# Feed-forward chunks 1 to 9 with the weights stationary and all 256 tokens moving

## The chip, the cores and the metric

One core of one Trainium2 chip. The metric is the device time of one execution in microseconds, as the median of several runs of the same program.

## The reference, cut to what matters

A two-layer decoder trunk on 256 tokens of width 1024. Four of its eight stages are half-step SwiGLU feed-forwards with an inner width of 2816, and these are what the change touches:

```python
def swiglu(x, w_gate, w_up, w_down):
    return (jax.nn.silu(x @ w_gate) * (x @ w_up)) @ w_down

x = layer_norm(DN_ALPHA * x + 0.5 * swiglu(x, ffn_w_gate[i, 0], ffn_w_up[i, 0], ffn_w_down[i, 0]),
               ln_g[i, 0], ln_b[i, 0])
```

The stages are, in order: feed-forward, attention (8 MoBA and 8 forgetting heads), feed-forward, gated input embedding; feed-forward, spatial gating unit (SGU), feed-forward, gated input embedding. All data are float32.

## The kernel before

**Numbers.** Products run in the `fp32r` format. To keep float32 accuracy each operand is split into a high part (ScalarE copies it into an `fp32r` tile) and a low part (VectorE subtracts the high part from the original), and each product is three matmuls: high with high, high with low, low with high (`product`, L332 to L334). This holds for activations (`xT_hi`, `xT_lo`), for h (`hT_hi`, `hT_lo`) and for every weight (`g_hi`, `g_lo`, `d_hi`, `d_lo`).

**Tiling of a feed-forward.** The inner width is cut into 11 chunks of 256 features (`NCH`, `FC`). For one chunk a weight tile of 1024 x 512 is loaded: 256 columns of the gate weight beside 256 of the up weight. It comes in two halves of the contraction (`rawA` for blocks 0 to 3, `rawB` for blocks 4 to 7), and the 256 x 1024 tile of the down weight comes into `rawD`. SyncE issues these loads in a fixed order and waits before each until VectorE has read the raw tile (`load_half`, `load_d`). The split weights have two slots each, so they are made one chunk ahead.

**One chunk on TensorE** (`chunk`, L436). Tokens are stationary: for each half h of 128 tokens, `up` runs 8 blocks x 3 matmuls with `xT` as weights of 128 x 128 and 512 moving columns (gate beside up) into PSUM bank `gu[h]`. So `gu[h]` is tokens by features. ScalarE takes silu of its first 256 columns (`gate`, L725), VectorE multiplies this by 0.5 and by the other 256 columns (`gated`, L995) into `stage`. The down product contracts over features, so h must be turned: `turn` transposes two blocks of 128 x 128 of `stage` into PSUM bank `tp[h]` (L385), ScalarE makes the high part from there (`hT_high`), VectorE the low part (`hT_low`), and `down` (12 matmuls of 512 columns for each half of the tokens) adds into `acc[h]`.

**Order.** All orders are written by hand, and semaphores tie the engines. On TensorE a chunk is

```python
up(c, cs, 0)
turn(c - 1, cs - 1, 1)
down(c - 1, cs - 1, 0)
up(c, cs, 1)
turn(c, cs, 0)
down(c - 1, cs - 1, 1)
```

so the down product runs one chunk behind. ScalarE runs, in a chunk: the high part of the next chunk's rawA, `gate` of half 0, `hT_high` of half 1 of the chunk before, the high part of rawD, that of rawB, `gate` of half 1, `hT_high` of half 0. VectorE runs in the same order the low parts and `gated`. Chunks 0 and 10 are partly written out: chunk 0 meets the end of the stage before, chunk 10 the layer norm behind it. Chunks 2 to 9 are hardware loops of two chunks each. In the second feed-forward of each layer, `p_tok` is transposed once, through the same `tp` banks.

**Counting.** `phase_bases` gives for each stage how often each semaphore has been raised before it; `turn` and `hT_high` compute their waits from these.

## Time and profile before

| | |
|---|---|
| median of 3 runs | 1067.05 us |
| lowest, highest run | 1065.72, 1068.27 us |
| span of the profiled execution | 1064.0 us |
| instructions | 12641 |
| mean granted clock of TensorE | 0.982 of full |
| HBM read | 189.90 MB, 179 GB/s over the span |

The profile is of one execution. Its span runs from the first to the last instruction and is 3.05 us below the median of the runs; the page gives no other time of that execution. PE is TensorE's matmuls, PEld its weight loads (recorded apart, since they overlap the matmuls), DVE VectorE, ACT ScalarE, POOL GpSimd, SP SyncE. L332 is line 332 of the kernel. Matmul ends are modelled and matmuls overlap, so what one costs in a stream is the distance from start to start, not its recorded duration.

### The profile page before, as it was taken

To read this page: it belongs to the slowest core of one execution; us is meant where nothing else is said; L and a number is where in the kernel's file an instruction comes from. 1 tells how busy PE (TensorE), PEld (TensorE's weight loads), DVE (VectorE), ACT (ScalarE), POOL (GpSimd) and SP (SyncE) were. 2 spreads that over 40 slices of the span, in tenths; PEclk is the share of its full clock that TensorE was granted. 3 is DMA by queue.
4 is the path that set the end of the run, shared out by engine and by line. 5 is a ranking of instruction groups with operands and counts; after the bars stand their busy time and mean duration, and the time that the engine had idled before them with its cause. 6 is when DMAs were issued, how large, how long until landed. Compare 5 with 4: busy or idle time off the path is not lost.

```text
span 1064.0 us, 12641 instructions
## 1 busy us (share of the span) xinstructions
PE 1044.0 (98%) x4770; PEld 856.1 (80%) x4770; DVE 610.9 (57%) x704; ACT 447.3 (42%) x515; POOL 39.4 (4%) x53
## 2 busy tenths in 40 slices
PE   7999999999999899999999999999999899999998
PEld 5888888787878688888888888888888788888886
DVE  4554455775434855445586554545678775454574
ACT  5434344345533553434435444344354454444441
POOL 2100000100000100000010000000110100000010
PEclk9999999999967999999999999999999999999999
DMA  8854656355312475565546755546266575654531
GB/s 281 286 197 158 207 179 207 116 161 160 118 41 70 173 271 198 160 212 181 183 170 222 249 178 183 197 158 209 87 208 236 178 258 192 203 188 167 197 119 40
DMA packets 128882, 191.46 MB, mean 180 GB/s; under 512 B 5288, under 2 KB 95400, under 8 KB 128720
## 3 DMA queue, kind: packets, MB, share of 16 engines
q1 hardware_dynamic: 125920, 180.37, 50.3%
q0 software_dynamic: 2928, 10.61, 3.0%
q8 instruction: 24, 0.39, 0.1%
q14 instruction: 10, 0.08, 0.0%
HBM read 189.90 MB, written 1.06 MB: 179 GB/s over the span
## 4 chain that ended last, share of the span: by engine, by line
PE 91%; DVE 4%; DMA 2%; ACT 1%; issue 1%; SPq 0%; POOL 0%; DVEq 0%
PE gu L332 19%; PE gu L334 19%; PE gu L333 19%; PE acc L332 9%; PE acc L334 9%; PE acc L333 9%; PE tp L385 4%; DVE g_lo L896 2%; PE acc L527 2%; ACT g_hi L675 1%; DMA rawB<-in_ffn_w_up 1%; DMA rawB<-in_sgu_w_in 1%; PE acc L524 1%; DMA rawB<-in_sgu_w_out 0%; DVE xT_lo L896 0%
## 5 line engine op out<-in xcount | busy, mean ns | idle before, releaser
L332 PE MATMUL gu<-g_hi,xT_hi 128*128 128x512 f32 x928 | 365.0, 393 | 5.9 <-DVE xT_lo L896 2.9
L334 PE MATMUL gu<-g_hi,xT_lo 128*128 128x512 f32 x928 | 362.2, 390 | 0.0
L333 PE MATMUL gu<-g_lo,xT_hi 128*128 128x512 f32 x928 | 361.8, 390 | 0.0
L332 PEld LDWEIGHTS gu<-g_hi,xT_hi 128*128 128x128 f32 x928 | 174.6, 188 | 43.5 <-DVE xT_lo L896 3.3
L334 PEld LDWEIGHTS gu<-g_hi,xT_lo 128*128 128x128 f32 x928 | 174.6, 188 | 36.6
L333 PEld LDWEIGHTS gu<-g_lo,xT_hi 128*128 128x128 f32 x928 | 174.8, 188 | 35.6 <-issue 0.2
L725 ACT ACTIVATE stage<-gu 128x256 f32<-128x256 f32 x88 | 33.8, 384 | 377.7 <-PE gu L334 377.7
L896 DVE TENSOR_TENSOR g_lo<-rawA,g_hi 128x2048 fp32r<-128x2048 f32 (+1 forms) x63 | 142.1, 2256 | 85.1 <-ACT g_hi L675 85.1
L896 DVE TENSOR_TENSOR g_lo<-rawB,g_hi 128x2048 fp32r<-128x2048 f32 x62 | 141.7, 2286 | 19.4 <-ACT g_hi L675 19.2
L995 DVE SCALAR_TENSOR_TENSOR stage<-stage,gu 128x256 f32<-128x256 f32 x88 | 37.0, 420 | 193.8 <-ACT stage L725 193.6
L332 PE MATMUL acc<-d_hi,hT_hi 128*128 128x512 f32 x352 | 144.4, 410 | 0.0
L675 ACT ACTIVATE g_hi<-rawA 128x2048 fp32r<-128x2048 f32 (+1 forms) x63 | 119.0, 1888 | 51.6 <-DMA rawA<-in_ffn_w_up 29.1
L334 PE MATMUL acc<-d_hi,hT_lo 128*128 128x512 f32 x352 | 138.0, 392 | 0.0
L333 PE MATMUL acc<-d_lo,hT_hi 128*128 128x512 f32 x352 | 137.7, 391 | 0.0
L896 DVE TENSOR_TENSOR d_lo<-rawD,d_hi 128x2048 fp32r<-128x2048 f32 x46 | 105.4, 2291 | 48.5 <-ACT d_hi L675 48.5
L675 ACT ACTIVATE g_hi<-rawB 128x2048 fp32r<-128x2048 f32 x62 | 118.6, 1913 | 11.4 <-DMA rawB<-in_ffn_w_up 5.1
L675 ACT ACTIVATE d_hi<-rawD 128x2048 fp32r<-128x2048 f32 x46 | 88.2, 1917 | 4.0 <-PE acc L334 2.6
L334 PEld LDWEIGHTS acc<-d_hi,hT_lo 128*128 128x128 f32 x352 | 66.1, 188 | 14.2
L333 PEld LDWEIGHTS acc<-d_lo,hT_hi 128*128 128x128 f32 x352 | 66.4, 189 | 11.5
L332 PEld LDWEIGHTS acc<-d_hi,hT_hi 128*128 128x128 f32 x352 | 66.2, 188 | 11.2
L1317 POOL TENSOR_TENSOR small<-small 128x1 f32<-128x1 f32 x14 | 18.0, 1287 | 940.2 <-DVE small L931 940.2
L896 DVE TENSOR_TENSOR hT_lo<-tp,hT_hi 128x256 fp32r<-128x256 f32 x88 | 36.9, 419 | 9.7 <-ACT hT_hi L675 9.7
(159 smaller groups left out, 703.7 us busy)
## 6 DMA issues: line engine op xcount, KB each, us to landing
rawD<-in_ffn_w_down SPq DMA_DIRECT2D x44, 1024.0 KB, 4.8
rawB<-in_ffn_w_gate SPq DMA_DIRECT2D x44, 512.0 KB, 4.1
rawB<-in_ffn_w_up SPq DMA_DIRECT2D x44, 512.0 KB, 5.3
rawA<-in_ffn_w_gate SPq DMA_DIRECT2D x43, 512.0 KB, 3.8
rawA<-in_ffn_w_up SPq DMA_DIRECT2D x43, 512.0 KB, 4.7
rawA<-in_attn_w_in SPq DMA_DIRECT2D x12, 512.0 KB, 4.4
rawB<-in_attn_w_in SPq DMA_DIRECT2D x12, 512.0 KB, 4.6
rawA<-in_ple_w_gate SPq DMA_DIRECT2D x8, 512.0 KB, 5.4
```

The lines of the kernel that those rows point to most:

```text
L332: pe.matmul(dst, hi[b], w_hi[b], start=first and b == 0, stop=False)
L333: pe.matmul(dst, hi[b], w_lo[b], start=False, stop=False)
L334: done = pe.matmul(dst, lo[b], w_hi[b], start=False, stop=last and b == len(hi) - 1)
L385: done = pe.transpose(tp[bank][0:src.shape[1], rows * q:rows * q + rows], src, ident[0:rows, 0:rows])
L524: pe.matmul(acc[0][:, sl, 0:S + P], sel_r[:, hh * P:hh * P + P], c_part[:, :], start=start, stop=False)
L527: done = pe.matmul(acc[0][:, sl, cols], qT[rows, blk, i_q * P:i_q * P + P], kT[rows, blk, 0:cols.stop - cols.start], start=g == 0, stop=g ...
L675: return act.activation(dst, src, ACT.Copy, scale=scale)
L725: act.activation(stage[:, h, 0:FC], gu[h][:, 0:FC], ACT.Silu).then_inc(act_done, 1)
L896: return dve.tensor_tensor(dst, src, hi.bitcast(F32), ALU.subtract)
L995: dve.scalar_tensor_tensor(out=stage[:, h, FC:2 * FC], in0=stage[:, h, 0:FC], scalar=0.5, in1=gu[h][:, FC:2 * FC], op0=ALU.mult, op1=ALU.m ...
L1317: pool.tensor_tensor(rstd[:, h:h + 1], var_eps[:, h:h + 1], neg_half, ALU.pow)\
```

## The change

In chunks 1 to 9 the roles in the first product are exchanged. The weights are stationary (128 of their columns at a time) and all 256 tokens move (`up_w`): `gu[0]` then holds the gate product and `gu[1]` the up product, each as two blocks of 128 features by 256 tokens. ScalarE takes silu of the whole `gu[0]` (`gate_w`), VectorE multiplies it by 0.5 and by `gu[1]` (`gated_w`) into `stage`, which is then features by tokens; the high and low parts of h are made from `stage` in SBUF (`hw_high`, `hw_low`) without a transpose. `up_w` runs 48 matmuls of 256 moving columns for each of its two calls in a chunk. Chunks 0 and 10 stay as they were. `hT_hi` and `hT_lo` have two slots of 256 tokens; `causal_c`, used in the attention alone, shares its place with `hT_hi`. The diff, cut to its core:

```diff
@@ -93,11 +92,11 @@
-    per = {"ffn": dict(g=NCH, d=NCH, u=NCH, t=NCH + 2, v=NCH + 2, a=2 * NCH, x=4, r=4, ln=1),
-           "attn": dict(g=8, d=0, u=6, t=5 + HEADS + 1 + 2, v=3, a=0, x=8, r=4, ln=1),
-           "sgu": dict(g=6, d=0, u=4, t=2 + 2, v=4, a=8, x=8, r=4, ln=2),
-           "ple": dict(g=2, d=1, u=2, t=2, v=2, a=4, x=4, r=0, ln=0)}
-    now = dict(g=0, d=0, u=0, t=2, v=2, a=0, x=0, r=0, ln=0)
+    per = {"ffn": dict(g=NCH, d=NCH, u=NCH, t=4, v=4, a=4, x=4, r=4, ln=1, hw=NCH - 2),
+           "attn": dict(g=8, d=0, u=6, t=5 + HEADS + 1 + 2, v=3, a=0, x=8, r=4, ln=1, hw=0),
+           "sgu": dict(g=6, d=0, u=4, t=2 + 2, v=4, a=8, x=8, r=4, ln=2, hw=0),
+           "ple": dict(g=2, d=1, u=2, t=2, v=2, a=4, x=4, r=0, ln=0, hw=0)}
+    now = dict(g=0, d=0, u=0, t=2, v=2, a=0, x=0, r=0, ln=0, hw=0)
     out = []
     for kind, _, s in PHASES:
         out.append(dict(now))
...
@@ -142,8 +141,13 @@
         xT_hi = sb("xT_hi", [P, KB, S], F32R)
         xT_lo = sb("xT_lo", [P, KB, S], F32R)
         stage = sb("stage", [P, HALVES, 512])
-        hT_hi = sb("hT_hi", [P, 3, 2, P], F32R)
-        hT_lo = sb("hT_lo", [P, 3, 2, P], F32R)
+        with ExitStack() as region:
+            hT_hi = sb("hT_hi", [P, 2, 2, S], F32R, region)
+        with ExitStack() as region:
+            causal_c = sb("causal_c", [P, 2, 384], where=region)
+        h_end = sb("h_tail", [P, 4 * S])
+        del h_end
+        hT_lo = sb("hT_lo", [P, 2, 2, S], F32R)
         pT_hi = sb("pT_hi", [P, HALVES, 2, P], F32R)
         pT_lo = sb("pT_lo", [P, HALVES, 2, P], F32R)
         gamma = sb("gamma", [P, D])
...
@@ -413,33 +417,50 @@
             for k, (kind, i, s) in enumerate(PHASES):
                 B = bases[k]
-                g0, d0, u0, t0, x0, a0 = (B[q] for q in ("g", "d", "u", "t", "x", "a"))
+                g0, d0, u0, t0, x0, a0, w0 = (B[q] for q in ("g", "d", "u", "t", "x", "a", "hw"))
                 if kind == "ffn":
...
                         g_product(g0 + c, (g0 + cs) % 2, h, gu[h][:, :], between=between)
-                    def turn(c, cs, h):
-                        pe.wait_ge(gu_taken[h], u0 + c + 1)
-                        transposes(h, t0 + c + p_use(s, cs, h), [stage[:, h, FC + P * b:FC + P * b + P] for b in range(2)])
+                    def up_w(c, cs, q):
+                        n, slot = g0 + c, (g0 + cs) % 2
+                        bank_free(q, u0 + c)
+                        for b in range(2):
+                            cols, dst = slice(FC * q + P * b, FC * q + P * b + P), gu[q][:, S * b:S * b + S]
+                            for kb in range(KB):
+                                if b == 0 and q == 0 and kb % 4 == 0:
+                                    pe.wait_ge((split_a, split_b)[kb // 4], n + 1)
+                                pe.matmul(dst, g_hi[:, slot, kb, cols], xT_hi[:, kb, :], start=kb == 0, stop=False)
+                                pe.matmul(dst, g_lo[:, slot, kb, cols], xT_hi[:, kb, :], start=False, stop=False)
+                                done = pe.matmul(dst, g_hi[:, slot, kb, cols], xT_lo[:, kb, :], start=False,
+                                                 stop=kb == KB - 1)
+                        done.then_inc(g_done, 1)
+                    def turn(n, h):
+                        pe.wait_ge(gu_taken[h], u0 + (1, NCH)[n])
+                        transposes(h, t0 + n * (1 + p_use(s)), [stage[:, h, FC + P * b:FC + P * b + P] for b in range(2)])
                     def down(c, cs, h, js=(0, 1)):
-                        pe.wait_ge(tp_taken[h], t0 + c + (2 if s == 2 and cs >= 1 else 1))
+                        if cs in (0, NCH - 1):
+                            pe.wait_ge(tp_taken[h], t0 + (1 if cs == 0 else 2 + p_use(s)))
+                        else:
+                            pe.wait_ge(hw_lo, w0 + c)
                         if k == 0 and cs == 0 and h == 1:
                             pe.wait_ge(bias_sb, 1)
-                        at = 2 if h == 1 and cs == NCH - 1 else h
-                        d_product(d0 + c, (d0 + cs) % 2, h, hT_hi[:, at], hT_lo[:, at], first=cs == 0,
-                                  last=cs == NCH - 1, js=js)
+                        tok = slice(h * P, (h + 1) * P)
+                        d_product(d0 + c, (d0 + cs) % 2, h, hT_hi[:, cs % 2, :, tok], hT_lo[:, cs % 2, :, tok],
+                                  first=cs == 0, last=cs == NCH - 1, js=js)
                     def chunk(c, cs):
-                        up(c, cs, 0)
-                        turn(c - 1, cs - 1, 1)
+                        up_w(c, cs, 0)
+                        if cs == 1:
+                            turn(0, 1)
                         down(c - 1, cs - 1, 0)
-                        up(c, cs, 1)
-                        turn(c, cs, 0)
+                        up_w(c, cs, 1)
                         down(c - 1, cs - 1, 1)
                     xT_wait(0, use)
...
@@ -468,17 +489,16 @@
                     c = NCH - 1
                     up(c, c, 0)
-                    turn(c - 1, c - 1, 1)
                     down(c - 1, c - 1, 0)
-                    turn(c, c, 0)
+                    turn(1, 0)
                     bank_free(1, u0 + c)
...
                     down(c - 1, c - 1, 1, (0,))
-                    turn(c, c, 1)
+                    turn(1, 1)
                     down(c - 1, c - 1, 1, (1,))
-                    use = (t0 + NCH + p_use(s, c, 0), t0 + NCH + p_use(s, c, 1) + 1)
+                    use = (t0 + 2 + p_use(s), t0 + 3 + p_use(s))
                     ln_turn(0, x0, use)
                     down(c, c, 1)
...
@@ -716,13 +737,21 @@
             for k, (kind, i, s) in enumerate(PHASES):
                 B = bases[k]
-                g0, d0, u0, t0, x0, a0 = (B[q] for q in ("g", "d", "u", "t", "x", "a"))
+                g0, d0, u0, t0, x0, a0, w0 = (B[q] for q in ("g", "d", "u", "t", "x", "a", "hw"))
                 last_phase = k + 1 == len(PHASES)
                 if kind == "ffn":
-                    def gate(c, h, value=None):
-                        act.wait_ge(g_done, 2 * c + (2 * g0 + h + 1))
+                    def gate(c, h):
+                        act.wait_ge(g_done, 2 * (g0 + c) + h + 1)
                         act.activation(stage[:, h, 0:FC], gu[h][:, 0:FC], ACT.Silu).then_inc(act_done, 1)
+                    def gate_w(c):
+                        act.wait_ge(g_done, 2 * c + (2 * g0 + 1))
+                        act.activation(stage[:, 0, :], gu[0][:, :], ACT.Silu).then_inc(gu_taken[0], 1)
+                    def hw_high(c, cs):
+                        act.wait_ge(gu_taken[1], u0 + c + 1)
+                        copy(hT_hi[:, cs % 2, :, :], stage[:, 1, :].rearrange("p (b t) -> p b t", b=2)).then_inc(hw_hi, 1)
                     def chunk(c, cs):
                         slot = (g0 + cs + 1) % 2
...
@@ -731,19 +760,25 @@
                         hi_g_into(c + (g0 + 1), slot, 0)
                         if k > 0 and cs == 0:
                             half1()
-                        gate(c, 0)
+                        if cs == 0:
+                            gate(c, 0)
+                        elif cs == 1:
+                            hT_high(1, 0, t0)
                         if cs > 0:
-                            hT_high(1, c + (t0 - 1 + p_use(s, cs - 1, 1)))
+                            gate_w(c)
                         hi_d(c + d0, (d0 + cs) % 2)
                         hi_g_into(c + (g0 + 1), slot, 1)
-                        gate(c, 1)
-                        hT_high(0, c + (t0 + p_use(s, cs, 0)))
+                        if cs == 0:
+                            gate(c, 1)
+                            hT_high(0, 0, t0)
+                        else:
+                            hw_high(c, cs)
                     chunk(0, 0)
...
                         for h in range(HALVES):
-                            act.wait_ge(tp_full[h], t0 + 3 - h)
+                            act.wait_ge(tp_full[h], t0 + 2)
                             copy(pT_hi[:, h, :, :], tp[h][:, 0:2 * P].rearrange("p (b t) -> p b t", b=2))\
                                 .then_inc(tp_hi[h], 1)
                     with act.Fori(0, (NCH - 3) // 2) as r:
...
@@ -985,16 +1019,28 @@
                 B = bases[k]
                 f0 = sum(kind in ("ffn", "ple") for kind, _, _ in PHASES[:k])
-                g0, d0, u0, t0, v0, a0, x0, r0, ln0 = (B[q] for q in ("g", "d", "u", "t", "v", "a", "x", "r", "ln"))
+                g0, d0, u0, t0, v0, a0, x0, r0, ln0, w0 = (
+                    B[q] for q in ("g", "d", "u", "t", "v", "a", "x", "r", "ln", "hw"))
                 last_phase = k + 1 == len(PHASES)
                 if kind == "ffn":
                     def gated(c, h):
-                        dve.wait_ge(act_done, 2 * c + (a0 + h + 1))
+                        dve.wait_ge(act_done, a0 + (2 if c else 0) + h + 1)
                         dve.scalar_tensor_tensor(out=stage[:, h, FC:2 * FC], in0=stage[:, h, 0:FC], scalar=0.5,
                                                  in1=gu[h][:, FC:2 * FC], op0=ALU.mult, op1=ALU.mult)\
                             .then_inc(gu_taken[h], 1)
+                    def gated_w(c):
+                        dve.wait_ge(gu_taken[0], u0 + c + 1)
+                        dve.wait_ge(g_done, 2 * c + (2 * g0 + 2))
+                        dve.scalar_tensor_tensor(out=stage[:, 1, :], in0=stage[:, 0, :], scalar=0.5, in1=gu[1][:, :],
+                                                 op0=ALU.mult, op1=ALU.mult).then_inc(gu_taken[1], 1)
+                    def hw_low(c, cs):
+                        dve.wait_ge(hw_hi, w0 + c)
+                        low(hT_lo[:, cs % 2, :, :], stage[:, 1, :].rearrange("p (b t) -> p b t", b=2),
+                            hT_hi[:, cs % 2, :, :]).then_inc(hw_lo, 1)
                     def chunk(c, cs):
                         slot = (g0 + cs + 1) % 2
...
@@ -1008,13 +1054,16 @@
                             if k > 0:
                                 half1()
                             gated(c, 0)
-                        if cs > 0:
-                            gated(c, 0)
-                            hT_low(1, c + (v0 - 1 + p_use(s, cs - 1, 1)))
+                        if cs == 1:
+                            hT_low(1, 0, v0)
                         lo_d(c + d0, (d0 + cs) % 2)
                         lo_g_into(c + (g0 + 1), slot, 1)
-                        gated(c, 1)
-                        hT_low(0, c + (v0 + p_use(s, cs, 0)))
+                        if cs == 0:
+                            gated(c, 1)
+                            hT_low(0, 0, v0)
+                        else:
+                            gated_w(c)
+                            hw_low(c, cs)
                     chunk(0, 0)
                     if k == 0:
```

## Rows read from the trace of the kernel before

**Rows 1.** The page: engine table, then the chain that ended last by engine

```profile
PE 1044.0 (98%) x4770; PEld 856.1 (80%) x4770; DVE 610.9 (57%) x704; ACT 447.3 (42%) x515; POOL 39.4 (4%) x53
...
PE 91%; DVE 4%; DMA 2%; ACT 1%; issue 1%; SPq 0%; POOL 0%; DVEq 0%
```

**Rows 2.** Stretches: a chunk, the attention heads (busy by engine, granted clock, DMA)

```profile
core 0: us, PE busy (x) PEld busy (x) DVE busy (x) ACT busy (x) POOL busy (x), PEclk, DMA share, GB/s
...
162.22:179.05 16.83, 16.83 (x78) 13.87 (x77) 8.30 (x8) 6.72 (x7) 0.00 (x0) 1.00 0.57 190
...
299.00:334.00 35.00, 34.95 (x123) 28.55 (x123) 11.94 (x51) 12.76 (x39) 0.00 (x0) 0.51 0.00 1
```

**Rows 3.** Groups by form, TensorE: busy us, mean ns of one | idle before

```profile
L332 PE MATMUL gu<-g_hi,xT_hi 128*128 128x512 f32 x928 | 365.0, 393 | 5.9 <-DVE xT_lo L896 2.9 <-DVE g_lo L896 2.9
...
L332 PE MATMUL acc<-d_hi,hT_hi 128*128 128x512 f32 x352 | 144.4, 410 | 0.0
...
L385 PE MATMUL tp<-ident,stage 128*128 128x128 f32 x208 | 38.2, 271 | 0.0
...
L332 PEld LDWEIGHTS gu<-g_hi,xT_hi 128*128 128x128 f32 x928 | 174.6, 188 | 43.5 <-DVE xT_lo L896 3.3 <-DVE g_lo L896 2.6 <-issue 2.1
```

**Rows 4.** In order of time, TensorE, one chunk: start us, us

```profile
162.22 0.39 PE L332 MATMUL gu<-g_hi,xT_hi 128*128 128x512 f32 x1
...
167.43 0.39 PE L334 MATMUL gu<-g_hi,xT_lo 128*128 128x512 f32 x1
...
168.11 0.39 PE L333 MATMUL acc<-d_lo,hT_hi 128*128 128x512 f32 x1
168.34 0.40 PE L334 MATMUL acc<-d_hi,hT_lo 128*128 128x512 f32 x1
168.58 0.39 PE L332 MATMUL acc<-d_hi,hT_hi 128*128 128x512 f32 x1
...
179.04 0.39 PE L332 MATMUL gu<-g_hi,xT_hi 128*128 128x512 f32 x1
```

**Rows 5.** In order of time, TensorE, forget-gate product

```profile
218.61 0.28 PE L332 MATMUL acc<-xT_hi,wf_hi 128*8 128x256 f32 x1
...
219.29 0.28 PE L332 MATMUL acc<-xT_hi,wf_hi 128*8 128x256 f32 x1
```

**Rows 6.** In order of time, weight loads: after a turn, and in the SGU

```profile
108.88 0.19 PEld L332 LDWEIGHTS acc<-d_hi,hT_hi 128*128 128x128 f32 x1
108.99 0.19 PEld L333 LDWEIGHTS acc<-d_lo,hT_hi 128*128 128x128 f32 x1
...
812.56 1.87 PEld L621 LDWEIGHTS acc<-v_sgu,ws_T 128*128 128x128 f32 x16
```

**Rows 7.** Groups by form, VectorE and ScalarE: 128x256 beside 128x512

```profile
L995 DVE SCALAR_TENSOR_TENSOR stage<-stage,gu 128x256 f32<-128x256 f32 x88 | 37.0, 420 | 193.8 <-ACT stage L725 193.6
...
L725 ACT ACTIVATE stage<-gu 128x256 f32<-128x256 f32 x88 | 33.8, 384 | 377.7 <-PE gu L334 377.7
...
L1072 DVE TENSOR_TENSOR stage<-stage,acc 128x512 f32<-128x512 f32 x8 | 5.5, 684 | 12.8 <-PE acc L334 7.9 <-ACT stage L781 4.9
...
L781 ACT ACTIVATE stage<-gu 128x512 f32<-128x512 f32 x8 | 4.8, 598 | 36.9 <-PE gu L334 36.9
```

**Rows 8.** In order of time: low parts of rawB, a third-phase chunk's first matmul

```profile
172.56 2.29 DVE L896 TENSOR_TENSOR g_lo<-rawB,g_hi 128x2048 fp32r<-128x2048 f32 x1
...
587.49 2.28 DVE L896 TENSOR_TENSOR g_lo<-rawB,g_hi 128x2048 fp32r<-128x2048 f32 x1
...
588.72 0.48 PE L332 MATMUL gu<-g_hi,xT_hi 128*128 128x512 f32 x1
```

**Rows 9.** In order of time, TensorE: scores of three attention heads

```profile
297.04 0.92 PE L527 MATMUL acc<-kT,qT 64*128 64x256 f32 x4
...
299.52 1.54 PE L527 MATMUL acc<-kT,qT 64*128 64x256 f32 x4
...
303.93 0.79 PE L527 MATMUL acc<-kT,qT 64*128 64x256 f32 x1
```

More of the change, by code:

```diff
@@ L456, in _ @@
                                   stop=True).then_inc(bias_mm, 1)
-                    turn(0, 0, 0)
+                    turn(0, 0)
                     chunk(1, 1)
@@ L461, in _ @@
                         for h in range(HALVES):
-                            transposes(h, t0 + 2 - h, [p_tok[:, h, P * b:P * b + P] for b in range(2)])
+                            transposes(h, t0 + 1, [p_tok[:, h, P * b:P * b + P] for b in range(2)])
                     with pe.Fori(0, (NCH - 3) // 2) as r:
```

33 lines of the change are left out of this document (16 added, 17 removed).

## The prediction

> **What bounds the kernel now.** I read the page first: its engine table gives TensorE 98% of a span of 1064.0 us, and the chain that ended last is 91% TensorE [rows 1]. A busy TensorE isn't TensorE at its peak, so the second view is the stretch view with the granted clock. In a whole feed-forward chunk the clock is full (2.4 GHz) and the engine never idle; only in the attention heads is about half of it granted (0.51, the 1.2 GHz level) [rows 2]. The groups by form give what the engine does: 928 triples of weight products and 352 triples of down products, each matmul 512 moving columns, and 208 transposes of `stage` [rows 3]. Their mean of 390 ns is not what one costs, since they overlap. So the fourth view is the order of time: one chunk from the first matmul of its up product at 162.22 to that of the next at 179.04 lasts 16.82 us, and the 24 matmuls of one up product start from 162.22 to 167.43, which is 5.21 / 23 = 0.2267 us from start to start [rows 4]. A chunk has 48 + 24 = 72 of these, 16.32 us. The remaining 0.50 us is its four transposes. One turn can be seen alone: the last up matmul starts at 167.43, two transposes follow, and the second down matmul starts at 168.11 [rows 4]. That is 0.68 us for what is two steps of 0.2267 without the turn, so a turn costs 0.23; twice that is 0.46, and the last 0.04 lies in the spacings of the down product behind it, up to 0.24 at 168.34 and 168.58 [rows 4]. There is no idle time in the chunk, so each nanosecond of TensorE's stream is a nanosecond of the span.
>
> **The change part by part.** Removed: chunks 1 to 9 have 18 of the 22 turns of a feed-forward phase; chunks 0 and 10 keep four. Nine chunks in each of four phases are 36, and 36 x 0.50 us = 18.0 us leave TensorE's stream. Nothing else hides there, so I count all of it.
>
> Changed: in those chunks 48 up matmuls of 512 moving columns become 96 of 256. The columns are the same, the weight loads double. Over the kernel 36 x 48 = 1728 matmuls become 3456. What a 256-column matmul in this number format costs can be read off the forget-gate product: its matmuls start at 218.61 and, six later, at 219.29, so 0.1133 us each [rows 5], exactly half of 0.2267. If that holds, 3456 x 0.1133 = 391.7 us take the place of 1728 x 0.2267 = 391.7, and the cost is nothing. But those matmuls load 8 weight columns, the new ones 128. What hides the load is the matmul before it, and that cover shrinks from 0.227 to 0.113 us. How fast can loads of 128 columns follow each other? The SGU's matmuls (128 moving columns) show it: sixteen loads span 1.87 us, and one lasts about 0.19, so (1.87 - 0.19) / 15 = 0.112 us from one to the next [rows 6]. After a turn, the load for the first down matmul starts at 108.88 and the next at 108.99, 0.11 us later, although such a load is recorded as 188 ns [rows 3, 6]. So the load just fits: 0.112 under 0.1133, with a margin of about one nanosecond. The low bound of the price is 0.1133, since half a 512-column matmul can't stream faster than it does now. The high bound, if a load must finish its recorded 188 ns before its matmul starts and the next load only starts with that matmul, is 0.188 us. Between these I take 0.1136, nearest to rows 5, as the two rates are too close for none of the pairs to slip: 3456 x 0.0003 = +1.0 us.
>
> Here a rule of the Trainium skill speaks against the change. The page Perfetto Trace Analysis, section Identifying the Most-Contended Engine, says to judge how near TensorE is to its limit by the busy share of its weight loads. That share is 80% [rows 1], and 1728 loads more of 188 ns would add 325 us to 856 us, more than the span. By it the loads would become the bound; the sum goes by the starts, which are closer together than the loads are long.
>
> VectorE and ScalarE: a chunk's two silu of 384 ns become one of about 598 (the 128x512 sigmoid row), its two gatings of 420 ns one of about 684 (a 128x512 product with PSUM); the two high copies and the two low parts of h shrink likewise, so each engine is some 0.3 us a chunk shorter [rows 7]. Neither engine is the bound. The path to h is new: after the second up product, gating, high copy, low part, about 0.68 + 0.60 + 0.68 = 2.0 us with hand-offs on top. The down product that needs it comes after the previous chunk's second down half (12 x 0.2267 = 2.7) and the next first up product (5.4), so 8.1 us cover it. ScalarE now waits for the gating ahead of its next high copy of weights, and VectorE for the high copy ahead of its next low part, some 1.5 us later than before. The first half's low part is ready before that of the second half starts at 172.56, for a chunk that begins at 179.04 [rows 4, 8], so at least 6.5 us early: it can take that. PSUM banks come free as before, since each is read within a microsecond and not rewritten for a half chunk. The loads that SP issues are the same in number and order; SP waits for the same low parts, and POOL's queue is untouched. The overlay of `causal_c` moves no instruction.
>
> One requirement comes sooner: the second half of the weights (rawB) is needed after 12 matmuls of the first up product, which is 2.72 us now and 1.36 us then. In a steady chunk the low part ends at 174.85 and is needed at 179.04 + 2.72 = 181.76, 6.9 us of slack [rows 8]. The tightest is chunk 1 of the third feed-forward phase: ready at 589.77, needed at 588.72 + 1.36 = 590.08, so 0.3 us remain [rows 8]. I cost this at nothing; were that cover gone, it would cost some tenths of a microsecond, four times at most.
>
> Sum: -18.0 + 1.0 = -17.0 us. The profiled execution spans 1064.0 us and so becomes 1047.0. The page gives no time of that execution beyond its span; the three timed runs have a median of 1067.05, 3.05 us over it, which I leave as it is: 1050.0 us, -1.6%.
>
> **The rivals.** (a) The loads slip a little. If the 17/16 by which moving columns fall short of 2.4 GHz (0.2267 us against 512 / 2.4 = 0.2133) also stretches a load, 0.112 becomes 0.117 us. That is 3456 x 0.0037 = 12.8 us given back: -18.0 + 12.8 gives 1061.9 us. For it: the margin is a nanosecond, and loads then run under every matmul. Against it: 0.112 was measured with loads and matmuls running together.
>
> (b) Slower: the weight load ends last at every pair. Its place is the hand-over from load to matmul in the 96 up matmuls of a chunk; the load starts only when the matmul before it has started, and every delay of it then shows. It decides from 18.0 us / 3456 = 5.2 ns a pair, at 0.1185 us. Spacings disturbed by this much exist: behind a turn down matmuls start 0.23 to 0.24 us apart instead of 0.2267 [rows 4]. If each pair had 7 ns more, it would be 0.120 us, +24.2 us: 1067.05 - 18.0 + 24.2 = 1073.2 us. Against it: with 512 columns a load has more than twice the cover, and the disturbed spacings still come only behind a turn, so they aren't the load's own length.
>
> (c) The loads bind at their recorded length: 3456 x (0.188 - 0.1133) = +258 us, 1307 us. Loads that follow each other in 0.11 us [rows 6] speak clearly against it. This is what the Trainium skill's rule (Perfetto Trace Analysis, Identifying the Most-Contended Engine) would mean here.
>
> (d) The gain is paid back elsewhere: the second half of the weights is late in every chunk, or the attention heads lose clock. A head starts 2.48 us after the one before at the full level (297.04 to 299.52) and 4.41 us at the half one (299.52 to 303.93) [rows 9]; the heads will now come 4.5 us earlier (nine chunks of the first phase), and the fall of the clock may catch one head more or fewer, 2 us either way. That belongs to the forecast's own range. As a rival, all of it together taking back 18 us, it gives about 1067 us; nothing speaks for it.
>
> **How the numbers follow.** Forecast 0.70, at 1046.5 to 1054 (2 us either way for the clock, 1.3 for the spread of the runs, and up to 1 ns a pair). Rival (a) 0.13, 1054 to 1065. Rival (b) 0.12. Rival (c) 0.02. Rival (d) 0.03, within 0.2%, which is about what a measurement of this kernel can tell from no change (2 us of 1067). A tail of (a) ends in that band too, so: faster 0.82, same 0.04, slower 0.14. The range 1046.5 to 1065 takes in the forecast and (a), and leaves (b), (c) and the edges out.
>
> **What the changed profile would show.** Right: 208 transposes of `stage` become 64; 96 matmuls of 128x256 in a chunk, starting 0.113 us apart; a chunk period of 16.3 us; 1728 loads more, whose busy share nears 100% without the span growing; VectorE idle before its gating until the second up product ends. Wrong: starts 0.117 us or more apart at full clock (a, b); gaps ahead of the 13th of the 256-column matmuls with VectorE's low part of rawB as releaser (d); a granted clock below 1.00 in feed-forward chunks.

## The result and the profile after

| | before | after |
|---|---|---|
| median | 1067.12 us (4 runs) | 1072.95 us (4 runs) |
| lowest, highest | 1065.72, 1068.27 us | 1071.73, 1075.38 us |
| ratio after / before, 95% interval | | 1.0069, 1.0051 to 1.0088 |
| span of the profiled execution | 1064.0 us | 1069.6 us |

The change makes the kernel 0.5 to 0.9% slower, where 1.6% faster was forecast. The page of the changed kernel, its engine table and its chain, answers to [rows 1]:

```profile
PE 1049.1 (98%) x6354; PEld 933.1 (87%) x6354; DVE 606.3 (57%) x632; ACT 442.5 (41%) x443; POOL 38.9 (4%) x53
...
PE 90%; DVE 5%; DMA 2%; issue 1%; ACT 1%; POOL 0%; SPq 0%; DVEq 0%; ACTq 0%
```

Little of the kernel waits anew: TensorE is still 98% busy and 90% of the chain. The weight loads rose from 80% to 87%, not towards 100%. So most of the loss must be inside TensorE's own stream. Groups by form (busy us, mean ns of one | idle before), against [rows 3]:

```profile
L437 PE MATMUL gu<-xT_hi,g_hi 128*128 128x256 f32 x1152 | 326.3, 283 | 1.2 <-DVE g_lo L930 1.2
...
L389 PE MATMUL tp<-ident,stage 128*128 128x128 f32 x64 | 10.9, 272 | 0.0
...
L437 PEld LDWEIGHTS gu<-xT_hi,g_hi 128*128 128x128 f32 x1152 | 220.8, 192 | 4.2 <-DVE g_lo L930 1.7
```

The 256-column matmuls are there, 3 x 1152. The idle time ahead of them is 1.2 us in the whole kernel. In order of time, the first and last of the 48 matmuls of one `up_w` call, then the first matmuls of two chunks that follow each other (start us, us), against [rows 4]:

```profile
103.66 0.28 PE L437 MATMUL gu<-xT_hi,g_hi 128*128 128x256 f32 x1
...
109.30 0.28 PE L439 MATMUL gu<-xT_lo,g_hi 128*128 128x256 f32 x1
...
112.16 0.28 PE L437 MATMUL gu<-xT_hi,g_hi 128*128 128x256 f32 x1
...
129.16 0.28 PE L437 MATMUL gu<-xT_hi,g_hi 128*128 128x256 f32 x1
```

From 112.16 to 129.16 the chunk period is 17.00 us, where 16.3 was forecast. The 48 matmuls start from 103.66 to 109.30: 5.64 / 47 = 0.120 us each, not 0.1136. Thirty-six chunks times (17.00 - 16.82) are 6.5 us.

There is one new wait, in chunk 1 of the second feed-forward and in the same way in that of the fourth. The 12th and 13th matmuls of the second feed-forward's chunk 1, and the low part of rawB that the 13th needs:

```profile
373.01 0.28 PE L439 MATMUL gu<-xT_lo,g_hi 128*128 128x256 f32 x1
373.90 0.39 PE L437 MATMUL gu<-xT_hi,g_hi 128*128 128x256 f32 x1 [0.61 <-DVE g_lo L930]
...
371.56 2.29 DVE L930 TENSOR_TENSOR g_lo<-rawB,g_hi 128x2048 fp32r<-128x2048 f32 x1
```

The low part ends at 373.85, and the 13th matmul starts 0.89 us after the 12th instead of 0.12. The fourth feed-forward loses 0.80 us in the same place, so the two waits cost 1.6 us. The spans differ by 5.6 us and not by 6.5 + 1.6, since other parts of the kernel became shorter: from the first feed-forward's last chunk to the second one's chunk 1, where the attention heads lie, it is 191.5 us (180.16 to 371.62) against 193.0 (179.04 to 372.01).

The path to h, in order of time on VectorE and ScalarE, and the first down matmul that reads it:

```profile
109.62 0.69 DVE L1037 SCALAR_TENSOR_TENSOR stage<-stage,gu 128x512 f32<-128x512 f32 x1 [1.57 <-PE gu L439]
...
110.34 0.63 ACT L695 ACTIVATE hT_hi<-stage 128x512 fp32r<-128x512 f32 x1 [5.02 <-DVE stage L1037]
...
111.00 0.69 DVE L930 TENSOR_TENSOR hT_lo<-stage,hT_hi 128x512 fp32r<-128x512 f32 x1 [0.70 <-ACT hT_hi L695]
...
117.92 0.40 PE L336 MATMUL acc<-d_hi,hT_hi 128*128 128x512 f32 x1
```

Gating, high copy and low part end at 111.69, 2.4 us after the last matmul of `up_w` started at 109.30. The down product that reads them begins behind the next `up_w`, at 117.92, another 6.2 us later. This part of the prediction held.

### The profile page after: what moved, and what is told of

Its sections match the earlier page's. It is cut to its first block, busy times and chain, and to the rows that moved or that the text cites. A ratio compares the mean times of both kernels' runs of the same rounds, so it can differ in the third digit from the quotient of the medians.

```text
span 1069.6 us, 15501 instructions
## 1 busy us (share of the span) xinstructions
PE 1049.1 (98%) x6354; PEld 933.1 (87%) x6354; DVE 606.3 (57%) x632; ACT 442.5 (41%) x443; POOL 38.9 (4%) x53
## 3 DMA queue, kind: packets, MB, share of 16 engines
HBM read 189.90 MB, written 1.06 MB: 179 GB/s over the span
## 4 chain that ended last, share of the span: by engine, by line
PE 90%; DVE 5%; DMA 2%; issue 1%; ACT 1%; POOL 0%; SPq 0%; DVEq 0%; ACTq 0%
PE gu L437 13%; PE gu L439 13%; PE gu L438 13%; PE acc L336 9%; PE acc L337 9%; PE acc L338 8%; PE gu L336 7%; PE gu L338 6%; PE gu L337 6%; PE tp L389 2%; DVE g_lo L930 2%; PE acc L547 1%; DMA rawB<-in_ffn_w_up 1%; DMA v_att<-bias_rows 1%; DVE x_tok L982 1%
## 5 line engine op out<-in xcount | busy, mean ns | idle before, releaser
L437 PE MATMUL gu<-xT_hi,g_hi 128*128 128x256 f32 x1152 | 326.3, 283 | 1.2 <-DVE g_lo L930 1.2
L439 PE MATMUL gu<-xT_lo,g_hi 128*128 128x256 f32 x1152 | 326.0, 283 | 0.0
L438 PE MATMUL gu<-xT_hi,g_lo 128*128 128x256 f32 x1152 | 325.9, 283 | 0.0
L437 PEld LDWEIGHTS gu<-xT_hi,g_hi 128*128 128x128 f32 x1152 | 220.8, 192 | 4.2 <-DVE g_lo L930 1.7
L438 PEld LDWEIGHTS gu<-xT_hi,g_lo 128*128 128x128 f32 x1152 | 220.9, 192 | 2.6
L439 PEld LDWEIGHTS gu<-xT_lo,g_hi 128*128 128x128 f32 x1152 | 220.8, 192 | 0.0
L336 PE MATMUL gu<-g_hi,xT_hi 128*128 128x512 f32 x352 | 140.5, 399 | 5.6 <-DVE xT_lo L930 2.9
L338 PE MATMUL gu<-g_hi,xT_lo 128*128 128x512 f32 x352 | 138.0, 392 | 0.0
L337 PE MATMUL gu<-g_lo,xT_hi 128*128 128x512 f32 x352 | 137.7, 391 | 0.0
L695 ACT ACTIVATE g_hi<-rawB 128x2048 fp32r<-128x2048 f32 x62 | 118.2, 1907 | 9.2 <-DMA rawB<-in_ffn_w_up 3.2
L338 PEld LDWEIGHTS gu<-g_hi,xT_lo 128*128 128x128 f32 x352 | 66.5, 189 | 14.3
```

What stands on the lines that cost most here:

```text
L336: pe.matmul(dst, hi[b], w_hi[b], start=first and b == 0, stop=False)
L337: pe.matmul(dst, hi[b], w_lo[b], start=False, stop=False)
L338: done = pe.matmul(dst, lo[b], w_hi[b], start=False, stop=last and b == len(hi) - 1)
L437: pe.matmul(dst, g_hi[:, slot, kb, cols], xT_hi[:, kb, :], start=kb == 0, stop=False)
L438: pe.matmul(dst, g_lo[:, slot, kb, cols], xT_hi[:, kb, :], start=False, stop=False)
L439: done = pe.matmul(dst, g_hi[:, slot, kb, cols], xT_lo[:, kb, :], start=False, stop=kb == KB - 1)
```

## The experiments

Each ratio is against runs of the kernel before on the same chip. e3, e4, e6 and e9 are one execution each and are read for the distances between starts alone.

**e1: tokens stationary again, no turning.** Only the first product of the changed kernel is put back; silu, gating and down product then take `gu` unturned, so the output means nothing.

```diff
-                        for b in range(2):
...
+                        tok = slice(q * P, (q + 1) * P)
+                        for kb in range(KB):
...
+                            done = product(gu[q][:, :], [xT_hi[:, kb, tok]], [xT_lo[:, kb, tok]],
+                                           [g_hi[:, slot, kb, :]], [g_lo[:, slot, kb, :]], kb == 0, kb == KB - 1)
```

> The changed kernel with the first product of chunks 1 to 9 put back to tokens stationary and 512 weight columns moving, while its new path without transposes stays: the two terms of the sum taken apart. What it leaves out is the turning of h: silu, gating and down product take gu as it comes, so the numbers mean nothing, but every operation of the changed kernel has its size. Theory A (the loss is the weight load under a 256-column matmul, 120.0 ns from start to start in the changed trace against 113.3, 3456 x 6.7 ns = 23.0 us): the load is hidden again, so the time is the changed kernel's less 23.0 us, 1072.95 - 23.0 = 1050.0 us, a chunk period of 16.32 us. Theory B (taking the transposes away did not give its 18.0 us, or the new path to h waits somewhere): 1055 us or more, with idle time ahead of the down products or a period over 16.5 us.

Measured: 1042.93 us, ratio 0.9789 (0.9768 to 0.9811), so 22.5 us faster than before, and 30 faster than the changed kernel, not 23. The first matmuls of two chunks that follow each other, in order of time:

```profile
100.24 0.39 PE L336 MATMUL gu<-g_hi,xT_hi 128*128 128x512 f32 x1
...
116.56 0.39 PE L336 MATMUL gu<-g_hi,xT_hi 128*128 128x512 f32 x1
```

The stretch from 290 to 345 us (the last three numbers are the granted clock, the share of the DMA engines and GB/s):

```profile
290.00:345.00 55.00, 52.98 (x237) 43.51 (x237) 28.68 (x79) 21.77 (x51) 1.00 (x1) 0.78 0.13 44
```

The period is 16.32 us, exactly the forecast: the transposes' 0.50 us a chunk did leave, 18.0 us in all, and no wait took their place. The spans of the two profiled executions, 1064.0 and 1039.4 us, differ by 24.6 us; most of the rest is the clock. The granted clock of the stretch above, which holds the attention heads, is 0.78; the same stretch has 0.69 in the kernel before and 0.72 in the changed one. Nine hundredths of 55 us at half speed are 2 x 0.09 x 55 = 9.9 us fewer at 1.2 GHz, and a head needs 2.48 us at full and 4.41 at half level [rows 9], so by estimate 9.9 us cost 9.9 x (1 - 2.48 / 4.41) = 4.3 us. 18.0 + 4.3 is 22.3 of the 24.6; from 10 to 25 us the granted clock is 1.00 here and 0.89 before, which can hold part of what is left. The medians differ less than the spans, because the clock also varies from run to run: over a whole execution it is 0.984 to 0.989 in the four runs of e1 and 0.978 to 0.984 in the 17 of the kernel before.

Against the changed kernel the chunks alone give 36 x (17.00 - 16.32) = 24.5 us, near the 23.0 of theory A, and the two waits of 1.6 us are gone. Six hundredths of granted clock are worth 2.9 us by the same estimate; that makes 29.0 of the 30. Theory B falls.

**e10: one thing alone.** The kernel before, with each 512-column matmul of the first product in chunks 1 to 9 split into two of 256. Nothing else changes.

```diff
+                        for b in range(2):
+                            half = slice(FC * b, FC * b + FC)
+                            for kb in range(KB):
...
+                                done = product(gu[h][:, half], [xT_hi[:, kb, tok]], [xT_lo[:, kb, tok]],
+                                               [g_hi[:, slot, kb, half]], [g_lo[:, slot, kb, half]],
+                                               first=kb == 0, last=kb == KB - 1)
```

> The kernel before with one thing alone: in chunks 1 to 9 each 512-column matmul of the first product becomes two of 256 columns (all 24 of the gate columns, then all 24 of the up columns). Tokens stay stationary, h is turned as before, the reference is computed. Theory E (each matmul carries about 13.3 ns beyond its columns at 2.4 GHz once 128 columns are loaded for it, in this orientation too): 120 ns from start to start, a chunk period of 16.83 + 48 x 0.0133 = 17.47 us, and 1728 x 0.0133 = 23.0 us more, 1088.5 to 1090 us. Theory of the prediction (time goes by columns alone, 113.3 ns): no change, 1066 to 1067 us.

Measured: 1085.48 us, ratio 1.0201 (1.0171 to 1.0231). The ratio stands for 21.4 us more, the medians (1066.19 us before on that chip) for 19.3. First and last of 48 matmuls, and the first of the next chunk:

```profile
105.43 0.28 PE L332 MATMUL gu<-g_hi,xT_hi 128*128 128x256 f32 x1
...
111.06 0.28 PE L334 MATMUL gu<-g_hi,xT_lo 128*128 128x256 f32 x1
...
122.88 0.28 PE L332 MATMUL gu<-g_hi,xT_hi 128*128 128x256 f32 x1
```

5.63 / 47 = 0.120 us, with tokens stationary and the weights moving; the period is 122.88 - 105.43 = 17.45 us, 0.63 over [rows 4] and 17.47 by theory E. Thirty-six times 0.63 are 22.7 us. The total is some 3 us under the 1088.5 expected: the two waits of 1.6 us are here too, but the granted clock from 290 to 345 us is 0.78 against 0.69, worth 4.3 us by the estimate in e1. 22.7 + 1.6 - 4.3 is 20.0, and the spans differ by 19.1 (1083.1 against 1064.0). The prediction's own theory, no change, falls. The split alone costs what the changed kernel lost. The roles of the operands have no part in it.

**e3: how it goes with the moving columns.** The number of columns that move differs by feed-forward phase.

```diff
+                                nm = {0: 128, 2: 192, 4: 320, 6: 384}[k]
+                                hi = xT_hi[:, :, :].rearrange("p k t -> p (k t)")[:, at:at + nm]
```

> One look at starts. In chunks 1 to 9 the number of moving columns differs by feed-forward phase: 128, 192, 320 and 384 in place of 256; what it leaves out or doubles are tokens, so the output means nothing. Theory A (a load of 128 columns takes about 117 ns from the start of the matmul before, whatever moves): 120 ns from start to start at 128 and 192 columns, and 141.7 and 170.0 ns at 320 and 384 (columns x 0.4427 ns, nothing added). Theory C (a fixed 6.7 ns a matmul on top of its columns): 63, 92, 148 and 177 ns. Theory D (the load is slowed by the columns that move beside it): about 112 ns at 128 columns, as the SGU's matmuls had it, and 120 at 192.

First and last of 48 matmuls, for each of the four widths:

```profile
100.58 0.22 PE L442 MATMUL gu<-xT_hi,g_hi 128*128 128x128 f32 x1
...
105.77 0.28 PE L444 MATMUL gu<-xT_lo,g_hi 128*128 128x128 f32 x1
...
439.84 0.25 PE L442 MATMUL gu<-xT_hi,g_hi 128*128 128x192 f32 x1
...
445.07 0.27 PE L444 MATMUL gu<-xT_lo,g_hi 128*128 128x192 f32 x1
...
665.45 0.30 PE L442 MATMUL gu<-xT_hi,g_hi 128*128 128x320 f32 x1
...
672.34 0.31 PE L444 MATMUL gu<-xT_lo,g_hi 128*128 128x320 f32 x1
...
969.45 0.33 PE L442 MATMUL gu<-xT_hi,g_hi 128*128 128x384 f32 x1
...
977.62 0.33 PE L444 MATMUL gu<-xT_lo,g_hi 128*128 128x384 f32 x1
```

So 5.19 / 47 = 0.110 and 5.23 / 47 = 0.111 us at 128 and 192 columns, 6.89 / 47 = 0.1466 at 320, 8.17 / 47 = 0.1738 at 384. From 256 columns (120.0 ns) to 512 (226.7 ns [rows 4]) each column adds 106.7 / 256 = 0.417 ns, one period of 2.4 GHz. Take off the columns at that rate (133.3 and 160.0 ns) and 13.3 and 13.8 ns are left at 320 and 384. At 512 it is 226.7 - 213.3 = 13.3 ns, at 256 it is 120.0 - 106.7 = 13.3 ns. From 256 to 512 columns one law fits all four widths, in streams of equal matmuls that load 128 columns each: **columns / 2.4 GHz plus 13.3 ns a matmul.** Theory A falls twice: the loads can follow each other in 0.111 us, less than 0.120, and at 320 and 384 the extra time is there although the load has ample cover. Theory C's form, a fixed cost on top, is right from 256 columns up, but with 13.3 ns over the columns at 2.4 GHz instead of 6.7 over columns of 0.4427 ns; below, starts follow the loads at 0.11 us. Theory D had that for 128 columns and missed it at 192, where it said 0.120.

**e4: how it goes with the loaded columns.** 256 columns move; 124, 120, 64 and (128, 64, 128) are loaded. Features are left out.

> One look at starts. In chunks 1 to 9, 256 columns move as in the changed kernel, but the number of stationary columns differs by feed-forward phase: 124, 120, 64, and in the last phase 128, 64, 128 over the three matmuls. The features of the columns left out are not computed. Theory A (the load is bound by its columns, some 0.83 to 0.89 ns each): 116.5 ns from start to start at 124 columns, 113.3 at 120 (load and moving columns level) and 113.3 at 64; in the last phase 113.3 into the matmul that loads 64, and 120 into the two that load 128. Theory C (fixed overhead): 120 ns in all four phases.

First and last of 48 matmuls in the first and third phase:

```profile
102.52 0.28 PE L440 MATMUL gu<-xT_hi,g_hi 128*124 128x256 f32 x1
...
108.03 0.28 PE L444 MATMUL gu<-xT_lo,g_hi 128*124 128x256 f32 x1
...
657.25 0.28 PE L440 MATMUL gu<-xT_hi,g_hi 128*64 128x256 f32 x1
...
662.58 0.28 PE L444 MATMUL gu<-xT_lo,g_hi 128*64 128x256 f32 x1
```

5.51 / 47 = 0.117 us at 124 loaded columns, and by the same count 0.117 at 120 (second phase) and 5.33 / 47 = 0.1135 at 64; the last phase, with one load in three of 64 columns, has 0.1166. So part of the fixed cost belongs to the load, and with 64 columns half of it is gone, as it was with the 8 columns of [rows 5]. But 120 and 124 columns cost the same, which a load bound by its columns would not: theory A has 0.1133 at 120. Theory C, 0.120 in all four phases, is wrong in all four.

**e6: roles, order, and few loaded columns.** By phase: tokens stationary with 256 weight columns moving; the same stationary twice in a row; 64 loaded and 512 moving; 32 loaded and 256 moving. Operands are left out or doubled.

> One look at starts, by feed-forward phase, in chunks 1 to 9 (the output means nothing: features, tokens or low parts are left out or doubled). First phase: tokens stationary again, but the weights move in pieces of 256 columns. Second: as in the changed kernel, the two products with the same stationary g_hi behind each other. Third: 64 stationary columns and 512 moving. Fourth: 32 stationary columns and 256 moving. Theory E (about 13.3 ns on top of columns / 2.4 GHz with 128 columns loaded, 6.7 with 64 or fewer, whatever moves): 120, 120, 220 and 113.3 ns from start to start. Theory G (the cost is tied to this orientation or to a change of weights): 113.3 ns in the first or in every third start of the second. Theory H (what a load adds shows only under short matmuls): 226.7 ns in the third.

The first two phases gave 0.120. First and last of 48 matmuls in the third and fourth:

```profile
710.42 0.40 PE L456 MATMUL gu<-g_hi 128*64 128x512 f32 x1
...
721.23 0.39 PE L456 MATMUL gu<-g_lo,g_hi 128*64 128x512 f32 x1
...
1026.22 0.28 PE L456 MATMUL gu<-xT_hi,g_hi 128*32 128x256 f32 x1
...
1031.75 0.28 PE L456 MATMUL gu<-xT_lo,g_hi 128*32 128x256 f32 x1
```

10.81 / 47 = 0.230 us, against 0.220 expected, and 5.53 / 47 = 0.118 against 0.113. Theories G and H fall. Theory E is right in the first two phases and wrong in the last two: fewer loaded columns do not always shorten the cost. With 256 moving, 32 were slower than 64, and with 512 moving, 64 (0.230) were slower than 128 (0.2267 [rows 4]).

**e9: data and banks.** By phase: no accumulation; moving tokens 16 columns later; two PSUM banks by turns; one and the same pair of operands throughout.

> One look at starts, by feed-forward phase, all with 128 columns loaded and 256 moving (the output means nothing). First phase: no accumulation, every matmul starts afresh in PSUM. Second: the moving tokens begin 16 columns later. Third: matmuls go by turns to a bank of gu and of tp. Fourth: every matmul loads the same 128 columns and moves the same 256. Theory E (the 120 ns belong to loading 128 columns under 256 moving ones, not to data or banks): 120 ns in all four. Theory L (adding to what the last matmul wrote costs it): 113.3 in the first and third. Theory M (the two reads of SBUF collide by address): other than 120 in the second or fourth.

0.120 us in the first, third and fourth phase. First and last of 48 matmuls in the first and second:

```profile
104.41 0.28 PE L449 MATMUL gu<-xT_hi,g_hi 128*128 128x256 f32 x1
...
110.05 0.28 PE L449 MATMUL gu<-xT_lo,g_hi 128*128 128x256 f32 x1
...
449.52 0.28 PE L449 MATMUL gu<-xT_hi,g_hi 128*128 128x256 f32 x1
...
455.09 0.29 PE L449 MATMUL gu<-xT_lo,g_hi 128*128 128x256 f32 x1
```

Neither adding to the last result nor the bank has a part, nor a change of operands, so theory L falls. Moving the read by 16 columns gives 5.57 / 47 = 0.1185 instead of 0.120: the place in SBUF counts, for about 1.5 ns. Theory M has that much right, and theory E, 0.120 throughout, misses it.

**e2, e5, e8: fewer matmuls for the same columns.** If each matmul has a fixed cost, the two that share g_hi should be one. It moves xT_hi beside xT_lo (512 columns); VectorE adds the halves of the bank.

```diff
-                                pe.matmul(dst, g_hi[:, slot, kb, cols], xT_hi[:, kb, :], start=kb == 0, stop=False)
-                                pe.matmul(dst, g_lo[:, slot, kb, cols], xT_hi[:, kb, :], start=False, stop=False)
-                                done = pe.matmul(dst, g_hi[:, slot, kb, cols], xT_lo[:, kb, :], start=False,
+                                pe.matmul(gu[b][:, :], g_hi[:, slot, kb, cols], xT_both[:, :, kb, :], start=kb == 0,
+                                          stop=False)
+                                done = pe.matmul(gu[b][:, 0:S], g_lo[:, slot, kb, cols], xT_hi[:, kb, :], start=False,
...
+                            dve.tensor_reduce(stage[:, q, S * b:S * b + S], gu[b][:, :].rearrange("p (r t) -> p t r", r=2),
+                                              AXX, ALU.add).then_inc(m_read, 1)
```

> A version that computes the reference: in chunks 1 to 9 the two products with g_hi become one matmul of 512 moving columns (xT_hi beside xT_lo in one tile), and the product with g_lo stays at 256 columns. A feature block takes a whole PSUM bank and VectorE adds its two halves (four reductions of 128x512 a chunk). Theory A (a load of 128 columns needs about 117 ns and shows only under a matmul of 256 columns): of three slots of 120 ns remain one of 120 and one of 226.7, 346.7 instead of 360.0 ns for each of 1152 triples, so 15.4 us less than the changed kernel: 1072.95 - 15.4 = 1057.6 us, faster than both. Theory C (every matmul of weights stationary carries 6.7 ns, whatever it moves): 120.0 + 233.3 = 353.3 ns, 1065.3 us. If VectorE with about 2.7 us more a chunk comes late, TensorE waits for banks and the time is above 1060 us under both.

Measured: 1066.49 us, ratio 1.0003 (0.9991 to 1.0016). Two of the pairs in order of time, with the first matmul of the pair after the third, and VectorE's reductions ahead of them and behind them:

```profile
107.49 0.40 PE L441 MATMUL gu<-xT_both,g_hi 128*128 128x512 f32 x1
107.72 0.28 PE L443 MATMUL gu<-xT_both,g_lo 128*128 128x256 f32 x1
107.84 0.40 PE L441 MATMUL gu<-xT_both,g_hi 128*128 128x512 f32 x1
108.08 0.28 PE L443 MATMUL gu<-xT_both,g_lo 128*128 128x256 f32 x1
...
108.55 0.40 PE L441 MATMUL gu<-xT_both,g_hi 128*128 128x512 f32 x1
...
102.49 0.69 DVE L1051 TENSOR_REDUCE stage<-gu 128x256 f32<-128x512 f32 x1 [1.57 <-PE gu L443]
...
110.10 1.47 DVE L1051 TENSOR_REDUCE stage<-gu 128x256 f32<-128x512 f32 x2
```

The group by form of the 512-column ones (busy us, mean ns | idle before, and for what):

```profile
L441 PE MATMUL gu<-xT_both,g_hi 128*128 128x512 f32 x1152 | 410.6, 399 | 3.1 <-DVE stage L1051 1.8 <-DVE g_lo L935 1.3
```

Three pairs take 1.06 us (107.49 to 108.55), so a pair takes 353 ns, not 346.7: better than the 360 of three matmuls, but the law doesn't hold for a mix. (The expectations below speak of 236.6 and 118.5 ns, 355 together; these are means over all calls and hold the waits of chunk 1 too.) Theory A falls. Theory C's 353.3 ns fit, but e3 has shown its sum wrong, so the right number speaks for nothing. TensorE also waited 1.8 us for VectorE's reductions in chunk 1 and 1.3 us for the low part of rawB.

e5 put the two runs of 256 columns next to each other in SBUF:

> The merged version again (it computes the reference), with xT_hi and xT_lo side by side for each block, so that the 512 moving columns are one contiguous run instead of two runs of 256. In the first merged version that matmul took 236.6 ns to the next start, not 226.7, and the 256-column one 118.5. Theory E (each matmul costs its columns at 2.4 GHz and about 13.3 ns on top when 128 columns are loaded for it; two separate runs in a moving operand cost 10 ns more): 226.7 + 120 = 346.7 ns a triple instead of 355, a chunk period of 16.5 us instead of 16.77, and 36 x 0.27 = 9.6 us less than the first merged version: about 1057 us. Theory F (the 236.6 comes from VectorE's reductions reading PSUM beside the matmuls, not from the operand's shape): no change, 1066 us.

Measured: 1067.32 us, ratio 1.0003 (0.9988 to 1.0018), with the distances of e2 within 0.1 ns. Theory E's part on two runs falls. Theory F has the right time, but e2's trace speaks against its cause: no reduction runs from 103.18 to 110.10, and the three pairs from 107.49 on take their 1.06 us all the same. e8 ordered the matmuls in groups of four of a kind, with the wait for the reductions in chunk 1 taken out (the 1.3 us for rawB stay):

> The merged version with the two kinds of matmul no longer alternating: four of 512 columns with g_hi, then four of 256 with g_lo, twice for each feature block. VectorE's first two reductions of chunk 1 also go ahead of its low part of rawA, since in the last version TensorE waited there 1.4 us in the first phase and 0.85 us in the second for a bank. It computes the reference. Theory I (the 236.5 ns of the 512-column matmul comes from standing between 256-column ones: the load for its successor and its own columns get in each other's way once for each change of size): inside a group 226.7 and 120 ns return, 346.7 on average, a chunk period of 16.5 to 16.6 us, and 6 to 10 us less with the two waits another 2 us less: 1056 to 1060 us. Theory K (the sum per 768 columns is what it is, 355 ns, however they are ordered): period 16.77, and only the waits are gained, 1065 us.

Measured: 1062.04 us, ratio 0.9963 (0.9945 to 0.9981). The first matmuls of two chunks that follow each other:

```profile
102.71 0.39 PE L443 MATMUL gu<-xT_both,g_hi 128*128 128x512 f32 x1
...
119.42 0.39 PE L443 MATMUL gu<-xT_both,g_hi 128*128 128x512 f32 x1
```

The period is 16.71 us, against 16.77 in e2 and 16.82 before. In steady chunks a 512-column matmul ahead of another takes 231.8 ns on average, against 235.8 in e2, and 256-column ones take 118.2. Theory I gets its direction, but 0.06 us of the 0.17 to 0.27 that it gave the period, and its time of 1056 to 1060 us was missed. It is the one version here that computes the reference and beats the kernel before, by 0.2 to 0.5%; by the two ratios it is about 1% under the changed one. 36 x (16.82 - 16.71) = 4.0 us come from the chunks. The eight runs lie between 1058 and 1064 us with the clock, the shorter ones at 0.985 and 0.986 and the longer at 0.980 to 0.984. The profiled execution is one of the short ones (0.78 granted in the heads' stretch). The median clock is 0.983 in both kernels, and the medians differ by 3.5 us, so the clock is no likely source of the gain; a run that separates the two was not made.

**e7: a mere shift.**

```diff
+                            if c == 0 and h == 0:
+                                pe.wait_ge(split_a, g0 + 1)
+                                for n in range(20):
+                                    pe.matmul(gu[h][:, :], xT_hi[:, 0, 0:P], g_hi[:, g0 % 2, 0, :], start=True,
+                                              stop=True)
```

> The kernel before with 20 matmuls of 512 columns more ahead of the attention's first product (they write a bank that the product overwrites), 20 x 0.2267 = 4.5 us. It asks what a mere shift of the attention heads does to the stretch at the lower clock, which lasted 34.1 us before, 30.7 in the changed kernel and 23.9 in the run without transposes. If the shift doesn't matter: 1065.5 to 1067.1 + 4.5, about 1070.8 us. If the stretch depends on when the heads come: up to 4.5 us less or more than that, with another length of the stretch in the profile.

Measured: 1069.30 us, ratio 1.0015 (1.0001 to 1.0028): 1.6 us more for 4.5 us of added work. The stretch from 290 to 345 us:

```profile
290.00:345.00 55.00, 54.95 (x237) 45.06 (x237) 24.24 (x78) 22.13 (x59) 0.00 (x0) 0.72 0.11 34
```

0.72 granted against 0.69: 2 x 0.03 x 55 = 3.3 us fewer at the lower level, worth 1.4 us by the estimate in e1. The profiled executions differ by 3.3 us (spans 1064.0 and 1067.3), which 4.5 - 1.4 = 3.1 explains. The medians differ by 2.2 us. There the clock of the runs fits: over a whole execution it is 0.984 to 0.986 in these ten runs and 0.977 to 0.984 in the 23 of the kernel before, with medians of 0.984 and 0.981, and 2 x 0.003 x 1065 = 6.4 us fewer at the lower level are worth 2.8 us, which leaves 1.7 of the 4.5. So work ahead of the heads can move the total by a few microseconds that have nothing to do with the edit. But the clock of one and the same kernel varies as much: the 23 runs of the kernel before lie between 1063.5 and 1070.5 us, the longest at the lowest clock.

## Why the prediction was wrong

- **The transposes**: 0.50 us a chunk, 18.0 us in all. Right (e1: 16.82 to 16.32 us).
- **The 256-column matmul**, the step that failed. The prediction found 0.1133 us in rows 5, called it "exactly half of 0.2267", and took time to go by columns alone. Two readings fit that row: no fixed cost, or a fixed cost that is smaller where 8 columns are loaded. The second is what the runs show: 0.120 us, not 0.1136, with 128 columns loaded. Rows 4 had the number for whoever read it as an amount: 0.2267 us for 512 columns is 0.2133 at 2.4 GHz and 13.3 ns more, and the prediction even used that difference, as a factor of 17/16 in rival (a), never as an amount. With 13.3 ns a matmul, 1728 more matmuls cost 23.0 us, and -18.0 + 23.0 = +5.0 us gives 1072.1; the chunk period has 0.04 us more than this (17.00 against 96 x 0.120 + 24 x 0.2267 = 16.96). The term was priced at 1.0 us. e10 shows it alone, 22.7 us in the chunks. Why a matmul has this fixed cost stays open.
- **The weight load's margin** (0.112 under 0.1133) was the wrong question. Loads do follow each other in 0.111 us (e3), and still the matmuls start 0.120 apart.
- **Rival (b)** had the number, 0.120 us and 1073.2 us, by luck, and not the mechanism: the load does not end last, for at 320 and 384 columns it has cover to spare and the same 13.3 ns appear. It was given 0.12, since only the disturbed spacings of rows 4 were asked to speak for it.
- **Rival (c)** fell. By the Trainium skill's rule on the busy share of weight loads (Perfetto Trace Analysis, Identifying the Most-Contended Engine) the change had little room, but the share is 87% in a kernel whose loads are not the bound. The prediction added 325 us of new loads to it; loads of 192 ns that start 120 ns apart overlap each other, and the busy time rose by 77 us. The Trainium skill's page TensorE: Matmul & The Clock Gate, section Back-to-back issue gap, gives the gap of a single matmul as its columns divided by 2.4 GHz plus 2.5 ns. The trace agrees with that form from 256 columns up; the constant is 13.3 ns here. For a stream with weight loads the same section has about 81 ns at 128 columns and 131 at 512; this case measured 110 and 226.7.
- **The path to h, the banks, ScalarE**: right, nothing waits.
- **The second half of the weights** was costed at nothing, and cost 1.6 us. The prediction took chunk 1 of the third feed-forward for the tightest. There the slack held. The waits are in the second and fourth, and rows of the kernel before that the prediction does not have show them coming. The low part of rawB and the first matmul of chunk 1 in the second feed-forward:

```profile
371.97 2.29 DVE L896 TENSOR_TENSOR g_lo<-rawB,g_hi 128x2048 fp32r<-128x2048 f32 x1
...
372.01 0.48 PE L332 MATMUL gu<-g_hi,xT_hi 128*128 128x512 f32 x1
```

  Ready at 374.26, needed at 372.01 + 1.36 = 373.37: 0.9 us late, not 0.3 us early. Rival (d) named this sign, a gap ahead of the 13th matmul, but for every chunk and 18 us.
- **The clock in the heads** was given 2 us either way. The stretch with the heads is 1.5 us shorter in the changed kernel, so this was wide enough; e1's profile differs by 4.3 us.

## What to carry to other kernels

Before splitting a matmul into narrower ones, divide its columns by the clock and subtract that from the distance between starts: what is left is paid once for every matmul, and the split pays it again. A row in which one more quantity differs (here 8 loaded columns instead of 128) can't show that there is no such cost. Where a saving is smaller than (matmuls added) x (that remainder), the change loses, however well everything else is hidden. And when a requirement comes sooner, its slack has to be read in every stage: here the stage called tightest had room, and two others did not.

## What was not expected of the hardware

- 256 to 512 moving columns cost columns / 2.4 GHz + 13.3 ns with 128 columns loaded for each matmul; 128 and 192 columns cost 0.110 to 0.111 us, the pace of the loads.
- The fixed part is not a simple function of the load: with 256 moving, 0.1133 us at 8 loaded columns, 0.118 at 32, 0.1135 at 64, 0.117 at 120 and 124, 0.120 at 128. A matmul of 512 columns costs more beside ones of 256 (235.8 ns in e2) or in groups that take turns with groups of them (231.8 ns in e8) than in a chunk of the kernel before (226.7). That kernel has such spacings too, for a while: in the chunk that starts at 389.31, right behind transposes, nine distances behind the first are 224 to 236 ns and the later ones 226.7. What sets these few nanoseconds stays open; e9 shows only that the place of the moving operand has a share in it.
- The stretch at 1.2 GHz in the attention heads differs between kernels that are alike in the heads and differ ahead of them: granted 0.69, 0.72 and 0.78 of full over the same 55 us. Since the clock also varies between runs of one kernel (0.977 to 0.984 over a whole execution), a single profile doesn't show how much of this belongs to where the heads fall.
